# First group's top-k steps behind later u rows, and even and odd attention heads in one step

## The chip, the cores and the metric

The kernel runs on 1 core of a Trainium2 chip. The metric is the device time of one launch in microseconds (us). About 0.5% of it, some 7.6 us, is what a measurement of this kernel can tell from no change.

## The reference

Two transformer-like blocks run one after the other on 256 tokens of width 1024, in float32. The change touches two places of the first block: its attention and the expert layer (`peer`).

```python
def first_block(x, ...):
    xn = rmsnorm(h, norm1_g[layer])
    proj = xn @ w_in[layer]
    q_a, k_a, v_a, q_r, f_r, i_r, g_r = jnp.split(proj, IN_SPLITS, axis=-1)
    attn = moba_attention(q_a, k_a, v_a)      # 8 heads of 64; one block of 256 keys: causal, with a linear bias
    rec = hgrn2(q_r, f_r, i_r, g_r, ...)      # gated recurrence, 4 heads of 128
    h = h + jnp.concatenate([attn, rec], axis=-1) @ w_out[layer]
    hn = rmsnorm(h, norm2_g[layer])
    h = h + peer(hn, peer_wq[layer], peer_subkeys[layer], peer_u[layer], peer_v[layer])

def peer(x, wq, subkeys, u, v):               # per token: 8 heads, 16 experts each
    s = einsum(x @ wq, subkeys)               # 2 x 128 scores for each head
    v1, i1 = top_k(s[:, :, 0], 16); v2, i2 = top_k(s[:, :, 1], 16)
    sc, p = top_k(v1[..., :, None] + v2[..., None, :], 16)
    eidx = take(i1 * 128 + i2, p); gates = softmax(sc)
    act = gelu(einsum(x, u[eidx]))
    return einsum(gates * act, v[eidx])
```

The second block (`second_block`) has a convolution/recurrence layer, an attention layer with 16 heads of 64, and two gated feed-forward layers. It follows the first and is not changed.

## The kernel before

Everything is written by hand for each engine: one program for SyncE (SP, loads of weights), GpSimd (POOL, gathers of expert rows), ScalarE (ACT), VectorE (DVE) and TensorE (PE). The order in which the lines stand is the order in which the engine works; semaphores join the engines.

**First block, attention.** The input projection runs in 14 units of 256 columns. From the ninth on, each unit is cut in halves (`slot_half(s)`, s = 16 to 27, at L1802 and L1805), and PE does other work behind each half. One is the recurrence (`level`, L1920). The other is attention in six steps: i = 0 to 3 for the queries 128 to 255 with two heads each, i = 4 and 5 for the queries 0 to 127 with four heads each. A step is `at_scores` (L1935, in half-unit s = 16 + i), `at_logits`, exponential and `at_norm` on DVE and ACT, `at_transpose` (L1946, s = 18 + i), a copy by ACT (`at_copy`), `at_out` (L1963, s = 20 + i) and `at_store` on DVE (L1215, L1218). Query and key have 64 features a head: an even head lies on partitions 0 to 63, an odd one on 64 to 127. `at_head(i, c)` says which head is the c-th of step i. Before the change all heads of one step have the same parity, so that all its score matmuls read one half of the partitions, all its output matmuls write one half, and its scores stand in one PSUM bank:

```python
return 4 * (i // 2) + i % 2 + 2 * c if i < 4 else (i - 4) + 2 * c
```

DVE also carries the modulation sums of the second block (`ada_ops`, L1098 and L1101) in between, whose weights SP loads (L416).

**End of the projection.** SP loads a unit's weights (L401) once PE is through with the unit four before. When unit 12 is done it starts a long run of loads: the output projection, the last modulation weights (L416), then the first expert query weights (L463), for which the first expert query matmul on PE (L2093) waits.

**Expert layer.** Tokens lie on partitions, 128 at a time (tt = 0, 1). For each of 256 (tile, head, k) one gather brings a row of u for each of the 128 tokens (512 KB), and DVE multiplies and sums it with the activations (`u_row`, L1396). A gather of v goes to PE (`v_row`, L2144), scaled by a diagonal matrix that ACT makes. The gathers are issued by POOL in the order `SEQ` (L540): u rows 0 to 37 first, then u row n and v row n - 38 in turn. They land in a ring of 16 slots, so POOL may be 16 ahead of the consumers (waits on `u_used`, `v_used`, `v_dve`).

The indices of the u rows come in groups of 32 (two heads) out of `top_rows` twice, `top_pairs` and `top_index` on DVE, whose input is the score batch that ACT copies from PSUM (`scores_in`, L732, semaphore `sc_in`). The indices of rows 0 to 31 are there before the row loop starts. Those of the next group (rows 32 to 63) are made between rows 0 and 31, and POOL waits for them at row 32 (`idx_ready`). The row loop calls the four steps behind fixed rows k of the group:

```python
if k == 6:  top_rows(gp + 2, 0, 2)
if k == 9:  top_rows(gp + 2, 2, 4)
if k == 12: top_pairs(gp + 2)
if k == 15: top_index(gp + 2)
```

## Time and profile before

| | us |
|---|---|
| median of 3 runs | 1530.38 |
| lowest and highest | 1525.65, 1531.63 |
| the profiled execution's own time | 1525.67 |
| its span from the first to the last instruction | 1523.8 |
| PE busy | 1366.5 |
| VectorE busy | 1025.8 |

The profile is of one execution, whose own time is close to the lowest of the three. All times in the rows are counted from its first instruction. The stages of the first block are, in that time: projection with recurrence and attention to about 152, output projection and expert queries to about 259 (with the first u rows from 206 on), the gathers of the expert layer to 868, then the second block to the end. "Idle before" in a timeline is idle time of that engine, and the arrow names what ended it.

### The profile page before, as it was taken

What the parts mean: (1) busy time and instruction counts of PE and PEld (TensorE: products, weight loads), DVE (VectorE), ACT (ScalarE), POOL (GpSimd) and SP (SyncE); (2) the same over time, 40 slices, a digit from 0 to 9 for tenths busy, and PEclk for the clock granted to TensorE, in tenths of its full rate; (3) what the DMA queues carried; (4) which work ended last, traced back from release to release, by engine and by line L of the source; (5) the groups of instructions that cost most, each with busy time, mean ns of one, the idle gap of its engine ahead of it and who ended that gap; (6) DMA issues with size and microseconds to landing.
All of it is one profiled execution on the core that took longest, in us unless ns stands there. A gap on an engine that the chain in (4) does not pass through costs nothing.

```text
span 1523.8 us, 20597 instructions
## 1 busy us (share of the span) xinstructions
PE 1366.5 (90%) x7648; PEld 1031.1 (68%) x7648; DVE 1025.8 (67%) x1830; ACT 503.0 (33%) x848; POOL 590.1 (39%) x630
## 2 busy tenths in 40 slices
PE   8999897788877777877788799999999998999998
PEld 7788896244422222322243399999999986999998
DVE  5896769968566676777544567778777467554454
ACT  2222212211111211231212074544445667444342
POOL 1320055777777777777777300022220003000000
PEclk9999999899999999999999999999999999999999
DMA  9865697999999999999999857688883441345540
GB/s 383 316 228 199 229 401 273 419 420 419 419 421 419 420 419 419 420 419 420 419 419 420 350 193 255 218 310 319 320 287 134 165 152 42 125 167 184 187 165 28
DMA packets 114078, 454.16 MB, mean 298 GB/s; under 512 B 12048, under 2 KB 29600, under 8 KB 100816
## 3 DMA queue, kind: packets, MB, share of 16 engines
q0 software_dynamic: 81616, 297.84, 48.8%
q1 hardware_dynamic: 32384, 155.31, 27.9%
q8 instruction: 45, 0.74, 0.2%
q14 instruction: 33, 0.27, 0.0%
HBM read 452.06 MB, written 1.05 MB: 297 GB/s over the span
## 4 chain that ended last, share of the span: by engine, by line
PE 52%; DMA 16%; POOL 12%; DVE 11%; issue 7%; ACT 2%; SPq 0%; DVEq 0%; POOLq 0%; ACTq 0%
PE psum L2253 16%; POOL arena L540 12%; DMA arena<-v_d,arena 10%; PE psum L1862 8%; PE psum L2267 8%; DMA arena<-u_d,arena 5%; DVE arena L1396 3%; PE psum L1818 3%; PE psum L1805 3%; PE psum L2144 2%; PE psum L1893 2%; PE psum L2093 1%; PE psum L1920 1%; PE psum L1877 1%; PE psum L2001 1%
## 5 line engine op out<-in xcount | busy, mean ns | idle before, releaser
L2144 PE MATMUL psum<-arena 128*128 128x512 f32 x952 | 470.1, 621 | 123.6 <-DMA arena<-v_d,arena 107.8
L2144 PEld LDWEIGHTS psum<-arena 128*128 128x128 f32 x952 | 164.6, 191 | 389.9 <-DMA arena<-v_d,arena 247.5
L1396 DVE CUSTOM_DVE_ANT_0 arena<-arena,psum 128x1024 f32<-128x1024 f32 x256 | 306.2, 1219 | 173.0 <-DMA arena<-u_d,arena 172.2
L540 POOL DMA_INDIRECT arena<-u_d,arena x256 | 243.9, 953 | 132.6 <-issue 54.9
L540 POOL DMA_INDIRECT arena<-v_d,arena x256 | 243.3, 950 | 78.1 <-issue 73.2
L1064 DVE TENSOR_TENSOR wlo<-ring,whi 128x2048 fp32r<-128x2048 f32 x69 | 158.1, 2292 | 86.4 <-ACT whi L608 86.4
L775 ACT ACTIVATE arena<-ident,arena 128x128 f32<-128x128 f32 x238 | 89.5, 397 | 353.3 <-PE psum L2144 315.6
L2253 PE MATMUL psum<-xh,whi 128*128 128x256 f32 x704 | 202.3, 287 | 1.6 <-DVE xl L1058 1.4
L2253 PE MATMUL psum<-xl,whi 128*128 128x256 f32 x704 | 199.4, 283 | 0.0
L2253 PE MATMUL psum<-xh,wlo 128*128 128x256 f32 x704 | 199.4, 283 | 0.0
L608 ACT ACTIVATE whi<-ring 128x2048 fp32r<-128x2048 f32 x69 | 131.3, 1903 | 23.6 <-PE psum L1862 18.9
L2253 PEld LDWEIGHTS psum<-xh,whi 128*128 128x128 f32 x704 | 135.1, 192 | 2.6 <-DVE xl L1058 1.8
L2253 PEld LDWEIGHTS psum<-xl,whi 128*128 128x128 f32 x704 | 135.2, 192 | 0.0
L2253 PEld LDWEIGHTS psum<-xh,wlo 128*128 128x128 f32 x704 | 135.1, 192 | 0.0
L555 POOL DMA_DIRECT2D second<-w_ada x64 | 46.3, 724 | 192.0 <-DVE second L1101 115.8
L1079 DVE TENSOR_TENSOR dlo<-ring,dhi 128x1024 fp32r<-128x1024 f32 x44 | 53.9, 1225 | 70.7 <-ACT dhi L624 70.7
L2267 PE MATMUL psum<-fh,dhi 128*128 128x256 f32 x352 | 99.8, 284 | 1.1 <-DVE fl L1644 1.1
L2267 PE MATMUL psum<-fh,dlo 128*128 128x256 f32 x352 | 99.8, 283 | 0.0
L2267 PE MATMUL psum<-fl,dhi 128*128 128x256 f32 x352 | 99.8, 283 | 0.0
L624 ACT ACTIVATE dhi<-ring 128x1024 fp32r<-128x1024 f32 x44 | 46.5, 1058 | 139.0 <-PE psum L2267 139.0
L1862 PE MATMUL psum<-xh,whi 128*128 128x256 f32 x256 | 75.0, 293 | 0.4 <-DVE xl L1058 0.4
L1862 PE MATMUL psum<-xh,wlo 128*128 128x256 f32 x256 | 72.4, 283 | 0.0
(310 smaller groups left out, 2301.0 us busy)
## 6 DMA issues: line engine op xcount, KB each, us to landing
ring<-w_ffn SPq DMA_DIRECT2D x44, 1536.0 KB, 6.8
second<-w_ada POOLq DMA_DIRECT2D x64, 384.0 KB, 6.1
arena<-w_ada SPq DMA_DIRECT2D x50, 384.0 KB, 6.9
ring<-w_inproj SPq DMA_DIRECT2D x14, 1024.0 KB, 7.6
ring<-w_qkv SPq DMA_DIRECT2D x12, 1024.0 KB, 4.9
ring<-w_l0in SPq DMA_DIRECT2D x10, 1024.0 KB, 5.8
ring<-w_peerq SPq DMA_DIRECT2D x6, 1024.0 KB, 8.2
sq<-w_ada SPq DMA_DIRECT2D x14, 384.0 KB, 6.5
```

The lines of the kernel that those rows point to most:

```text
L540: g.indirect_dma_start(S["rows"][:, p % GRING, :], None, u_d if kind == "u" else v_d, bass.IndirectOffsetOnAxis(S["idx"][:, n // SLOTS, n ...
L555: g.dma_start(ada2_slot[i % ADA2_RING].rearrange("p (u c) -> p u c", u=2), ada_weights(1, i)).then_inc(ada2_in[i % ADA2_RING], 16)
L608: a.activation(r32(S[f"whi{g % 2}"]), slot(g, 0, 2048), ACT.Copy).then_inc(w_hi, 1)
L624: a.activation(r32(S[f"dhi{j % 2}"]), slot(g, 2048, 3072), ACT.Copy).then_inc(d_hi, 1)
L775: a.activation(S["diag"][:, c % DIAGS, :], ident[:, :], ACT.Copy, scale=S["wts"][:, n // SLOTS, n % SLOTS:n % SLOTS + 1]).then_inc(diag_re ...
L1064: v.tensor_tensor(r32(S[f"wlo{g % 2}"]), slot(g, 0, 2048), S[f"whi{g % 2}"], ALU.subtract).then_inc(w_lo, 1)
L1079: v.tensor_tensor(r32(S[f"dlo{j % 2}"]), slot(g, 2048, 3072), S[f"dhi{j % 2}"], ALU.subtract).then_inc(d_lo, 1)
L1396: v.tensor_tensor_reduce(row, row, xrow[n // SLOTS], 1.0, 0.0, ALU.mult, ALU.add, S["act"][:, n // SLOTS, n % SLOTS:n % SLOTS + 1]).then_i ...
L1862: ins = t.matmul(bank[g % 2][:, b * T:(b + 1) * T], w(i, b, k), r32((hi, lo)[j][:, k, :]), start=(b == 0 and k == 0 and i + j == 0), stop= ...
L2144: ins = t.matmul(vacc[tt][:, at], S["diag"][:, c % DIAGS, :], row[:, at], start=(n % SLOTS == 0), stop=(n == LAST_PE[tt]))
L2253: ins = t.matmul(bank[g % 2][:, b * T:(b + 1) * T], r32(w[i][:, b, k, :]), r32((xh, xl)[jj][:, k, :]), start=(b == 0 and k == 0 and i + jj ...
L2267: ins = t.matmul(bank[2 + n // 2][:, 256 * (n % 2):256 * (n % 2) + 256], r32(w[i][:, n, :]), r32(S[f"{('fh', 'fl')[jj]}{u % 2}"]), start=( ...
```

## The change

Two things are done.

1. The rows behind which the four top-k steps stand come from a table: (15, 17, 19, 21) for the first group, and (6, 9, 12, 15), as before, for the others.
2. Attention steps take even and odd heads together: step i < 4 the heads 2i and 2i + 1, steps 4 and 5 the heads 0 to 3 and 4 to 7. Scores of even heads go to bank 4 and those of odd heads to bank 5, the transposes to bank 6, the outputs to bank 7. `at_store` copies all 128 partitions at once. The output projection's transposes no longer wait for ACT's last copy. The bias table is laid out from `at_head` as well.

```diff
+TOP_AT = ((15, 17, 19, 21), (6, 9, 12, 15))
...
-    return 4 * (i // 2) + i % 2 + 2 * c if i < 4 else (i - 4) + 2 * c
+    return 2 * i + c if i < 4 else 4 * (i - 4) + c
...
-                a.activation(flat(S[f"PT{i % 2}"]), bank[5][:, :], ACT.Copy).then_inc(at_pt, 1)
+                a.activation(flat(S[f"PT{i % 2}"]), bank[6][:, :], ACT.Copy).then_inc(at_pt, 1)
...
+            def by_parity(ap, i):
+                return ap.rearrange("p (j c n) -> p c j n", c=2, n=T if i < 4 else P)
+
+            def at_banks(i):
+                n = T if i < 4 else P
+                return psum[:, 2048:3072].rearrange("p (c x) -> p c x", c=2)[:, :, 0:T].rearrange(
+                    "p c (j n) -> p c j n", n=n)
...
-                v.tensor_tensor(S[f"L{b}"], bank[4][:, :], S["alibi"][:, i, :], ALU.add).then_inc(at_l, 1)
+                v.tensor_tensor(by_parity(S[f"L{b}"], i), at_banks(i), by_parity(S["alibi"][:, i, :], i), ALU.add
+                                ).then_inc(at_l, 1)
...
-                    v.tensor_copy(S["cat"][p0:p0 + 64, c:c + 2, P:T],
-                                  bank[6][p0:p0 + 64, 0:T].rearrange("p (a t) -> p a t", a=2)).then_inc(at_cat, 1)
+                    v.tensor_copy(S["cat"][:, i, P:T], bank[AT_OUT][:, 0:P]).then_inc(at_cat, 1)
...
-                    v.tensor_copy(S["cat"][p0:p0 + 64, 0:4, 0:P],
-                                  bank[6][p0:p0 + 64, :].rearrange("p (a t) -> p a t", a=4)).then_inc(at_cat, 1)
+                    c = 2 * (i - 4)
+                    v.tensor_copy(S["cat"][:, c:c + 2, 0:P],
+                                  bank[AT_OUT][:, 0:T].rearrange("p (a t) -> p a t", a=2)).then_inc(at_cat, 1)
...
-                    if k == 6:
+                    at = TOP_AT[gp > 0]
+                    if k == at[0]:
                         top_rows(gp + 2, 0, 2)
...
-                    ins = t.matmul(bank[4][:, c * n:(c + 1) * n], S["qa"][p0:p0 + 64, h // 2, q0:q0 + P],
+                    at = c // 2 * n
+                    ins = t.matmul(bank[4 + c % 2][:, at:at + n], S["qa"][p0:p0 + 64, h // 2, q0:q0 + P],
...
-                for c in range(2 if i < 4 else 4):
-                    h = at_head(i, c)
-                    for kt in range(2 if i < 4 else 1):
-                        ins = t.matmul(bank[6][p0:p0 + 64, c * P:(c + 1) * P], S["va"][:, kt, h * HD:(h + 1) * HD],
+                for kt in range(2 if i < 4 else 1):
+                    for c in range(2 if i < 4 else 4):
+                        h = at_head(i, c)
+                        p0, at = 64 * (h % 2), c // 2 * P
+                        ins = t.matmul(bank[AT_OUT][p0:p0 + 64, at:at + P], S["va"][:, kt, h * HD:(h + 1) * HD],
...
                 if tt == 0:
                     pe.wait_ge(at_l, 6)
-                else:
-                    pe.wait_ge(at_pt, 6)
```

DVE in the row loop of the expert layer, before the change, from u row 5 to u row 8. A row is one instruction; `row_in5` is the semaphore of the ring slot in which u row 5 lands, and `sc_in` that of the score batch; MAX and what follows it are `top_rows`:

```order
L1396 ISA arena<-arena,psum 128x1024 [waits row_in5]
L1396 ISA arena 128x1
L1396 ISA arena<-arena,psum 128x1024 [waits row_in6]
L1396 ISA arena 128x1
L1305 MAX arena<-arena 128x8 [waits sc_in]
L1305 MAX arena<-arena 128x8
L1309 MATCH_REPLACE arena<-arena 128x128 [waits dve_seq]
L1310 MAX_INDEX arena<-arena 128x8
L1309 MATCH_REPLACE arena<-arena 128x128
L1311 MAX_INDEX arena<-arena 128x8
L1314 MAX arena<-arena 128x8 [waits dve_seq]
L1314 MAX arena<-arena 128x8
```

The same engine and loop after the change, from u row 14 on:

```order
L1408 ISA arena<-arena,psum 128x1024 [waits row_in14]
L1408 ISA arena 128x1
L1408 ISA arena<-arena,psum 128x1024 [waits row_in15]
L1408 ISA arena 128x1
L1317 MAX arena<-arena 128x8 [waits sc_in]
L1317 MAX arena<-arena 128x8
L1321 MATCH_REPLACE arena<-arena 128x128 [waits dve_seq]
L1322 MAX_INDEX arena<-arena 128x8
```

The wait for the scores has moved from behind u row 6 to behind u row 15.

PE at the end of attention, before: the transposes of the recurrence's result in front of the output projection, the second tile's with a wait for ACT's last attention copy (`at_pt`):

```order
L1989 MATMUL psum<-ident,arena 128x128 [waits at_l,rec_row]
L1989 MATMUL psum<-ident,arena 128x128 x3
L1989 MATMUL psum<-ident,arena 128x128 [waits at_pt,rec_row]
```

The same place after:

```order
L2001 MATMUL psum<-ident,arena 128x128 [waits at_l,rec_row]
L2001 MATMUL psum<-ident,arena 128x128 x3
L2001 MATMUL psum<-ident,arena 128x128 [waits rec_row]
```

Only that wait is gone. In the attention steps themselves PE has the same instructions, in the same places and with the same waits; what differs is the half of the partitions and the bank that each uses, which such rows don't show.

## Rows read from the trace of the kernel before

**Rows 1.** the page: busy time of the matmul engine; GB/s moved in 40 slices
```profile
PE 1366.5 (90%) x7648; PEld 1031.1 (68%) x7648; DVE 1025.8 (67%) x1830; ACT 503.0 (33%) x848; POOL 590.1 (39%) x630
...
GB/s 383 316 228 199 229 401 273 419 420 419 419 421 419 420 419 419 420 419 420 419 419 420 350 193 255 218 310 319 320 287 134 165 152 42 125 167 184 187 165 28
```

**Rows 2.** chain of waits, 80 to 165 us: start, duration, what
```profile
85.93 1.06 PE psum L1935 x4
...
109.64 1.08 PE psum L1935 x8
110.73 1.02 PE psum L1963 x8
...
141.83 1.02 PE psum L1963 x8
...
145.72 6.92 PE psum L1805 x32
...
157.55 14.07 DMA arena<-w_peerq
```

**Rows 3.** stretches: window, sum of busy time, then PE, PEld, DVE, ACT, POOL, clock, DMA
```profile
82.00:122.00 40.00, 40.00 (x224) 33.74 (x223) 37.59 (x64) 13.02 (x40) 10.13 (x7) 1.00 0.58 211
82.00:152.00 70.00, 70.00 (x403) 59.96 (x402) 56.54 (x90) 18.32 (x49) 13.14 (x8) 1.00 0.55 200
142.00:172.00 30.00, 26.13 (x203) 24.96 (x202) 20.37 (x33) 9.82 (x21) 1.13 (x2) 1.00 0.98 371
254.00:868.00 614.00, 490.37 (x1190) 198.98 (x1190) 411.74 (x935) 128.41 (x304) 456.34 (x480) 0.98 1.02 414
```

**Rows 4.** timeline of TensorE in the second block: two heads together, then one alone
```profile
1241.27 0.71 PE L2310 MATMUL psum<-second 64*128 64x256 f32 x4
...
1242.12 0.39 PE L1893 MATMUL psum<-whi,xh 128*128 128x256 f32 x1
...
1249.91 0.70 PE L2310 MATMUL psum<-second 64*128 64x256 f32 x2
...
1250.76 0.48 PE L2336 MATMUL psum<-second 128*128 128x256 f32 x1
```

**Rows 5.** timelines of the attention stage and its end: DVE, PE, SP, PE
```profile
122.33 3.16 DVE L1208 TENSOR_SCALAR arena<-arena 128x128 f32<-128x128 f32 x4
...
128.32 0.60 PE L1946 MATMUL psum<-ident,arena 128*128 128x128 f32 x4
...
141.86 0.34 SPq L401 DMA_DIRECT2D ring<-w_outproj  x1
...
171.66 4.57 PE L2093 MATMUL psum<-xn,arena 128*128 128x128 f32 x24 [3.87 <-DMA arena<-w_peerq]
```

**Rows 6.** timeline of VectorE, first group of u rows: the wait for scores
```profile
214.23 0.08 DVE L1396 DVE_READ_ACCUMULATOR2_ANT arena<- 128x1 f32 x1
224.34 0.49 DVE L1305 MAX8 arena<-arena 128x8 f32<-128x128 f32 x2 [10.03 <-ACT arena L732]
```

**Rows 7.** chain of waits, 224 to 261 us: runs of u rows between top-k steps
```profile
227.22 3.51 DVE arena L1396 x6
...
233.53 3.51 DVE arena L1396 x6
...
242.00 3.51 DVE arena L1396 x6
...
250.88 10.28 DVE arena L1396 x18
```

**Rows 8.** timeline of GpSimd, which issues the gathers
```profile
253.93 0.94 POOL L540 DMA_INDIRECT arena<-u_d,arena  x1 [5.67 <-DVE arena L1396]
255.17 0.94 POOL L540 DMA_INDIRECT arena<-u_d,arena  x1 [0.30 <-issue]
```

**Rows 9.** DMA view, us to landing: u row 15 (issued 210.23), u row 17 (212.72)
```profile
arena<-u_d,arena POOLq DMA_INDIRECT x1, 14.2
...
arena<-u_d,arena POOLq DMA_INDIRECT x1, 16.8
```

More of the change, by code:

```diff
@@ L94 @@
 LEVELS = [128, 64, 32, 16, 8, 4, 2, 1]
+AT_OUT = 7
 def at_head(i, c):
-    return 4 * (i // 2) + i % 2 + 2 * c if i < 4 else (i - 4) + 2 * c
+    return 2 * i + c if i < 4 else 4 * (i - 4) + c
 def build(nc, xT, cols_d, w_d, alibi_d, masks_d, ident_d, tri_d, blk_d, sbmask_d, iota_d, subk_d, rg_d,
@@ L1211, in at_store @@
                 dve.wait_ge(at_o, i + 1)
-                p0 = 64 * (i % 2)
                 if i < 4:
-                    c = 2 * (i // 2)
-                    v.tensor_copy(S["cat"][p0:p0 + 64, c:c + 2, P:T],
-                                  bank[6][p0:p0 + 64, 0:T].rearrange("p (a t) -> p a t", a=2)).then_inc(at_cat, 1)
-                else:
-                    v.tensor_copy(S["cat"][p0:p0 + 64, 0:4, 0:P],
-                                  bank[6][p0:p0 + 64, :].rearrange("p (a t) -> p a t", a=4)).then_inc(at_cat, 1)
+                    v.tensor_copy(S["cat"][:, i, P:T], bank[AT_OUT][:, 0:P]).then_inc(at_cat, 1)
+                else:
+                    c = 2 * (i - 4)
+                    v.tensor_copy(S["cat"][:, c:c + 2, 0:P],
+                                  bank[AT_OUT][:, 0:T].rearrange("p (a t) -> p a t", a=2)).then_inc(at_cat, 1)
             AT_P = [0, 2, 4, 6, 8, 12, 16]
@@ L1480, in _ @@
                 if gp < 7:
-                    if k == 6:
+                    at = TOP_AT[gp > 0]
+                    if k == at[0]:
                         top_rows(gp + 2, 0, 2)
-                    if k == 9:
+                    if k == at[1]:
                         top_rows(gp + 2, 2, 4)
-                    if k == 12:
+                    if k == at[2]:
                         top_pairs(gp + 2)
-                    if k == 15:
+                    if k == at[3]:
                         top_index(gp + 2)
@@ L1945, in at_transpose @@
                 for c in range(4):
-                    ins = t.transpose(bank[5][:, c * P:(c + 1) * P], S[f"P{i % 2}"][:, c * P:(c + 1) * P],
+                    ins = t.transpose(bank[6][:, c * P:(c + 1) * P], S[f"P{i % 2}"][:, c * P:(c + 1) * P],
                                       ident[:, :])
@@ L1958, in at_out @@
                 pt = S[f"PT{i % 2}"]
-                p0 = 64 * (i % 2)
-                for c in range(2 if i < 4 else 4):
-                    h = at_head(i, c)
-                    for kt in range(2 if i < 4 else 1):
-                        ins = t.matmul(bank[6][p0:p0 + 64, c * P:(c + 1) * P], S["va"][:, kt, h * HD:(h + 1) * HD],
+                for kt in range(2 if i < 4 else 1):
[3 more added lines that the diff above has]
+                        ins = t.matmul(bank[AT_OUT][p0:p0 + 64, at:at + P], S["va"][:, kt, h * HD:(h + 1) * HD],
                                        pt[:, 2 * c + kt if i < 4 else c, :], start=(kt == 0), stop=(i >= 4 or kt == 1))
```

## The prediction

> **What bounds the kernel now.** I read the page first, then the chain of waits, then the stretches, and only then the timelines of the two places that the change touches. The page [rows 1] shows TensorE busy for 90% of the span, but the rate at which data moves tells more: from the eighth slice on it stands at 419 to 421 GB/s for 15 slices. That is the expert layer. Between 254 and 868 us the DMA engines are busy all the time [rows 3], and GpSimd issues a gather of 512 KB every 1.24 us [rows 8]. This stretch is a stream: it takes as long as its gathers take, and it starts when the first gather after the last hole is issued. That gather is the one of u row 32, at 253.93 [rows 8]. The seventh slice, 229 to 267 us, with 273 GB/s shows the hole before it.
>
> The attention stage is another matter. In 82 to 152 us TensorE is busy 70.00 of 70.00 us at full clock [rows 3], and the chain of waits runs over it without a break [rows 2]: projection halves, recurrence, scores (L1935), outputs (L1963). When the projection ends, the chain goes over to the load of the first query weights, 14.07 us [rows 2], and TensorE then stands idle for 3.87 us until they are there [rows 5]. Whatever TensorE saves before 152 us starts these loads sooner. The second block follows the stream by data alone and has no clock of its own, so what is won in front stays won.
>
> **The change, part one: the top-k steps.** VectorE ends u row 6 at 214.31 and waits until 224.34 for the scores that ScalarE copies [rows 6]: 10.03 us. Rows 7 to 15 could be worked on meanwhile. A row takes 10.28 / 9 = 1.14 us [rows 7]. After the change rows 7 to 15 would end at 214.3 + 9 x 1.14 = 224.6, but row 15 lands only at 210.23 + 14.2 = 224.4 [rows 9] and so ends at 225.6. The scores are there by then. The four steps take what they take now, read between the runs of rows [rows 6, 7]: 227.22 - 224.34 = 2.88, then 233.53 - 230.73 = 2.80, 242.00 - 237.04 = 4.96, and 250.88 - 245.51 = 5.37 us. So: first step to 228.5; row 16; row 17, which lands at 212.72 + 16.8 = 229.5 [rows 9], to 230.8; second step to 233.6; two rows to 235.9; third step to 240.8; two rows to 243.1; last step to 248.5. Now it ends at 250.88. The index is 2.4 us earlier, not 10, because six more rows (6.9 us) stand in front of it and row 15 lands 1 us late.
>
> The gather of row 32 gains more than its index. It now also waits for 18 rows to be used, which is so at 250.88 + 2 x 1.14 = 253.2, and starts at 253.93. After the change 22 rows are used before the index is there; the gather starts about 0.3 us behind it (the idle time between two gathers, [rows 8]), at 248.8. That is **5.1 us** earlier. The nearest bounds: 2.4 us if the gather follows its index only as late as it does now (some 3 us), and 6.1 us if row 15 is not waited for. I take the middle value, since it has the landings in it. The gathers of rows 22 to 31 come earlier too, and fill the time until about 247 us; they stand behind rows 12 to 21 in the same queue and delay none of them. The loads of the last query weights share the DMA engines with them; nothing in the chain of waits waits for those loads. What follows the index does not hurt: rows 22 to 31 have landed, and VectorE ends row 31 at 260 instead of 269, so that TensorE gets its first scaled v row sooner, which nothing waits for.
>
> **Part two: even and odd heads together.** A pair of score matmuls on different halves of the partitions can run side by side, and the trace has such a pair. In the second block two heads' scores, one on each half, take from 1241.27 to 1242.12, 0.85 us; one head alone takes from 1249.91 to 1250.76, also 0.85 us [rows 4]. The second head is free. Now the attention steps: a score step of two heads is 4 matmuls of 256 columns in 1.06 us, one of four heads 8 of 128 columns in 1.08 us, an output step 8 in 1.02 us [rows 2]. A matmul of 256 columns costs 6.92 / 32 = 0.216 us [rows 2], one of 128 half of it. If half of them are free, a step loses 0.43 us. Scores: 6 x 0.43 = 2.6 us. Outputs: 6 x 0.43 = 2.6 us, but here the two heads share the rows of the array and differ in columns, and no row of this trace shows two such matmuls side by side. Bounds: nothing, or all 2.6. I take all of it, from the nearest row, the pair of scores. TensorE then leaves the stage **5.2 us** sooner. All but the last output step lies before 141.86, where SP starts the run of loads [rows 5]; the run starts 4.8 us sooner, and keeps the DMA engines 98% busy to its end [rows 3]. I take **5.0 us** for the arrival of the query weights. The rest costs nothing: the logits have as many elements from two banks as from one, the copies of `at_store` get shorter (half the elements a partition), and the wait that is dropped was not last.
>
> Beside this stands a page of the Trainium skill, "TensorE: Matmul & The Clock Gate", section "Part 3: Packing small matmuls — row/col tiling", which gives 2.38x for three column tiles. As an estimate from that page, two tiles at the same share of the ideal would give 1.6x, and the outputs 2.0 us instead of 2.6. No row here shows it, and the sum goes without it.
>
> Is VectorE in the way? It is busy 56.54 of 70 us in the stage [rows 3]. The narrowest place that I found is the transpose of step 5: it starts at 128.32, and VectorE is through with its input at 122.33 + 3.16 = 125.49 [rows 5], a margin of 2.8 us. TensorE has by then won 0.43 x 9 = 3.9 us, so VectorE must follow by 1.1 us. Its idle time between 82 and 122 is 40 - 37.59 = 2.4 us [rows 3] and part of this is a wait for TensorE. It just fits; if it did not, up to 1.1 us of the 5.0 would be lost.
>
> **Sum.** 5.1 + 5.0 = 10.1 us. Against the profiled execution: 1525.67 - 10.1 = 1515.6. Its time is 4.7 us below the median of the three runs, so for the median I say 1530.38 - 10.1 = **1520.3 us**.
>
> **Rivals.**
> (a) Outputs do not overlap: only 2.6 us from part two, 7.7 in all, 1522.7. For it: no row shows it. Against: the scores do it fully.
> (b) VectorE or the loads take the bound in the attention stage, and part two gives some 3.5 instead of 5.0: 8.6 in all, 1521.8. For it: the margin of 2.8 us above. Against: VectorE has idle time, and waits for TensorE in this stage more than the other way round.
> (c) The u rows 12 to 17 land later than now, or the index is late, and the gather of row 32 gains only its 2.4 us: 7.4 in all, 1523.0. Row 15 already lands when it is wanted.
> (d) Slower: each change from one half of the array to the other costs a drain. The place is the attention steps. Heads alternate 1 time in four score steps, 3 times in two, and 3 times in each output step, 28 times in all. Going into a 64-wide step and out of it costs 0.85 - 2 x 0.216 - 2 x 0.108 = 0.20 us [rows 2, 4]. At 0.20 us for each of 28 alternations and nothing overlapped, part two costs 5.6 us; against 5.1 gained it ends at 1530.9, 0.5 us above the median. It decides from 0.18 us an alternation. Against it: the pair of scores pays nothing for its alternation [rows 4]. A page of the Trainium skill bears on this, "TensorEngine Tiling (Array Packing)", section "Key Properties": changing the tiling mode drains the engine, changing the tile alone does not. By that rule (d) is out, and the pair in the trace, with its 0.85 us, agrees.
> (e) Part one does nothing, since something other than the index holds gather 32: 5.0 in all, 1525.4. Against it: GpSimd was idle for 5.67 us before that gather, and what ended it was VectorE's work on the rows [rows 8], which part one moves forward.
>
> **How the numbers follow.** Forecast 0.60, (a) 0.15, (b) 0.11, (c) 0.07, (d) 0.03, (e) 0.04. The three runs before spread over 6 us, so a median is good to about 3 us. The range has the forecast with both upper bounds (6.1 + 5.2, less 4 of spread) at its lower end, 1515, and case (e) with some spread at its upper end, 1527. What a measurement can tell from no change is 0.5%, 7.7 us, that is a time under 1522.7. The forecast passes it in most draws, (b) in most, (a) and (c) in half or fewer: faster 0.64, same 0.33, slower 0.03.
>
> **What the profile after would show.** VectorE runs rows 0 to 15 without the wait of 10 us; the first MAX8 comes near 225.6 less the 5 us of part two. The gather of row 32 is issued about 10.1 us before 253.93, near 243.8. Score steps on TensorE take about 0.63 us and output steps 0.6; the first query weights land near 166.6 and the second block starts 10 us sooner. Output steps of 1.0 us would mean (a), idle time of TensorE between 82 and 152 (b), waits of VectorE for u rows 12 to 17 (c), score steps over 1.1 us (d). The prediction is wrong if the stream after row 32 is longer than the 614 us of now, which nothing in the change would explain.

## The result

The changed kernel takes 1516.93 us (median of 7 executions, 1512.38 to 1520.33), the kernel before, run beside it, 1527.67 us (7 executions, 1525.06 to 1531.63). The ratio is 0.9928, with a 95% interval of 0.9913 to 0.9944, which is 11.0 us less (8.6 to 13.3) and more than the 7.6 us that a measurement can tell from no change. The forecast was 10.1 us less and 1520.3 us, so faster, by both parts of the change. A second comparison on another occasion (run e8 below) gave 0.9913 [0.9893, 0.9932].

The profiled execution of the changed kernel has a span of 1517.1 us, where the kernel before had 1523.8. That is only 6.7 us. Why it is less than the medians say the prediction did not see; it has a section of its own below.

The page of the changed kernel, the lines that answer to [rows 1]:

```profile
PE 1364.3 (90%) x7648; PEld 1026.5 (68%) x7648; DVE 1025.8 (68%) x1830; ACT 503.1 (33%) x848; POOL 587.3 (39%) x630
...
GB/s 384 313 234 234 222 419 336 419 420 413 418 421 419 419 420 419 420 420 420 419 419 420 293 215 274 221 320 313 320 270 125 167 136 32 125 167 190 183 166 28
```

TensorE has the same 7648 matmuls and 2.2 us less busy time, and the seventh slice of the span moved 336 GB/s instead of 273: the hole in front of the stream is smaller. The chain of waits through the attention stage, with start, duration and what, answers to [rows 2]:

```profile
86.17 0.63 PE psum L1949 x4
...
108.19 0.65 PE psum L1949 x8
108.83 0.59 PE psum L1977 x8
...
137.34 0.59 PE psum L1977 x8
...
140.80 6.92 PE psum L1818 x32
...
152.85 14.01 DMA arena<-w_peerq
```

A score step of two heads fell from 1.06 to 0.63 us, one of four from 1.08 to 0.65, and an output step from 1.02 to 0.59. The projection half has its 6.92 us as before, and the load of the first query weights is issued at 152.85 instead of 157.55. The stretches, for [rows 3]:

```profile
82.00:122.00 40.00, 40.00 (x247) 33.31 (x246) 38.52 (x68) 13.50 (x40) 10.14 (x8) 1.00 0.60 214
82.00:147.00 65.00, 65.00 (x405) 55.11 (x404) 54.04 (x89) 18.20 (x48) 10.97 (x8) 1.00 0.60 214
244.00:858.00 614.00, 497.19 (x1210) 202.93 (x1210) 408.03 (x927) 129.02 (x305) 455.14 (x480) 0.99 1.02 414
```

TensorE is still busy for all of 82 to 147 us, so nothing of what it saved went into a wait. VectorE went from 37.59 to 38.52 of the first 40 us. From 244 to 858 us the DMA engines are busy all the time, as they were from 254 to 868; from the gather of row 32 to the last gather it takes 601.2 us, before 601.6. Next the timelines of the changed kernel, one engine each: SyncE where the run of loads at the end of the projection begins, TensorE's first query step, VectorE's first and last instruction of the top-k chain, and GpSimd's gathers of u rows 0, 31 and 32 (in brackets the idle time before, and what ended it).

```profile
137.37 0.34 SPq L404 DMA_DIRECT2D ring<-w_outproj  x1
```

```profile
166.91 5.47 PE L2105 MATMUL psum<-xn,arena 128*128 128x128 f32 x32 [4.03 <-DMA arena<-w_peerq]
```

```profile
220.57 0.48 DVE L1317 MAX8 arena<-arena 128x8 f32<-128x128 f32 x2
...
243.39 0.18 DVE L1382 CAST arena<-arena 128x32 int32<-128x32 f32 x1
```

```profile
185.07 1.03 POOL L543 DMA_INDIRECT arena<-u_d,arena  x1 [31.48 <-DVE arena L1382]
...
225.36 0.94 POOL L543 DMA_INDIRECT arena<-u_d,arena  x1 [0.30 <-issue]
243.84 0.94 POOL L543 DMA_INDIRECT arena<-u_d,arena  x1 [17.55 <-DVE arena L1382]
```

The first MAX8 comes at 220.57, which was forecast as 225.6 less the 5 us of part two. The index is ready at 243.58, and the gather of row 32 starts 0.26 us behind it, at 243.84, where 243.8 was forecast and 253.93 stood before [rows 8].

### The profile page after: what moved, and what is told of

Same layout as the page of the kernel before. It is cut to its first block, busy times and chain, and to the rows that moved or that the text cites. A ratio compares the mean times of both kernels' runs of the same rounds, so it can differ in the third digit from the quotient of the medians.

```text
span 1517.1 us, 20596 instructions
## 1 busy us (share of the span) xinstructions
PE 1364.3 (90%) x7648; PEld 1026.5 (68%) x7648; DVE 1025.8 (68%) x1830; ACT 503.1 (33%) x848; POOL 587.3 (39%) x630
## 4 chain that ended last, share of the span: by engine, by line
PE 49%; DMA 20%; DVE 11%; POOL 10%; issue 7%; ACT 1%; SPq 1%; DVEq 0%; POOLq 0%; ACTq 0%
PE psum L2265 16%; POOL arena L543 10%; DMA arena<-u_d,arena 10%; PE psum L1875 9%; PE psum L2279 8%; DMA arena<-v_d,arena 7%; DVE arena L1408 4%; PE psum L1818 3%; PE psum L2156 2%; PE psum L1906 2%; DMA arena<-w_ada 1%; PE psum L1933 1%; PE psum L2105 1%; PE psum L2013 1%; PE psum L1815 1%
## 5 line engine op out<-in xcount | busy, mean ns | idle before, releaser
L611 ACT ACTIVATE whi<-ring 128x2048 fp32r<-128x2048 f32 x69 | 131.3, 1902 | 23.7 <-PE psum L1875 18.9
```

The source lines that it names most:

```text
L611: a.activation(r32(S[f"whi{g % 2}"]), slot(g, 0, 2048), ACT.Copy).then_inc(w_hi, 1)
```

## The experiments

All kernels ran beside the kernel before; a median stands against that of before in the same comparison. Absolute times of two profiles can't be subtracted to better than some 3 us, since the profiled executions reach the attention stage at different times: the first score step starts at 84.07 us in one of the 14 profiles (e4) and at 87.25 in another (e10). Two distances are used instead. One is from the first score step to the first query step on TensorE: 85.8 us in both profiles of the kernel before, 80.5 to 81.2 wherever even and odd heads go together and nothing is added in between. The other is from the gather of u row 0 to that of row 32 on GpSimd: 64.1 us in each of the three profiles with the old top-k rows, 58.8 in the profile of the changed kernel. The second one is not fixed: over the seven profiles with the top-k steps behind rows 15, 17, 19 and 21 it goes from 58.6 to 60.2 us (58.8 after, 59.5 in e8, 60.2 in e5, 58.6 to 58.9 in the others), and what varies is how long VectorE waits for rows 13 to 15 to land.

### Each part alone

e1 is the kernel before with the first part alone:

```diff
+TOP_AT = ((15, 17, 19, 21), (6, 9, 12, 15))
...
-                    if k == 6:
+                    at = TOP_AT[gp > 0]
+                    if k == at[0]:
                         top_rows(gp + 2, 0, 2)
```

> The kernel before with the first change alone: the top-k steps of the first group stand behind u rows 15, 17, 19 and 21, the attention steps are as before. Theory 1 (the two parts add, and the first is worth what its wait for row 15's landing takes away): the gather of u row 32 starts at 248.6 us of the profile instead of 253.93, the gather of row 0 stays at 189.8, and the time is 5.1 to 5.4 us under before (ratio 0.9966). Rival (the first part only pays since the gathers start 4.75 us earlier in the changed kernel, with other landings): the gather of row 32 moves by under 3 us, and the time by under 3 us. If before loses TensorE clock in the second block's attention in some executions, this kernel has both levels of time too.

e2 is the changed kernel without it:

```diff
-TOP_AT = ((15, 17, 19, 21), (6, 9, 12, 15))
+TOP_AT = ((6, 9, 12, 15), (6, 9, 12, 15))
```

> The changed kernel with the first group's top-k steps back behind u rows 6, 9, 12 and 15: only the attention with even and odd heads together is left of the change. Theory 1: score steps 0.63 to 0.65 us and output steps 0.59 us as in the changed kernel, gather of row 0 at 185.1 us, gather of row 32 at about 249.2 us (4.75 us before 253.93), time 4.7 to 5.2 us under before (ratio 0.9968). Rival (without the later rows the top-k chain waits for the landings of row 15 in another way, and eats part of it): gather of row 32 at over 251 us, time under 3 us below before.

e1 took 1523.11 us against 1529.35 (ratio 0.9956 [0.9942, 0.9971], so 6.7 us less, 4.4 to 8.9), e2 1524.92 (0.9978 [0.9963, 0.9993], 3.4 us less, 1.1 to 5.7). The timelines of GpSimd with the gathers of rows 0 and 32, e1 first, then e2:

```profile
188.57 1.03 POOL L542 DMA_INDIRECT arena<-u_d,arena  x1 [31.21 <-DVE arena L1372]
...
247.44 0.94 POOL L542 DMA_INDIRECT arena<-u_d,arena  x1 [17.64 <-DVE arena L1372]
```

```profile
183.69 1.03 POOL L543 DMA_INDIRECT arena<-u_d,arena  x1 [31.70 <-DVE arena L1382]
...
247.79 0.93 POOL L543 DMA_INDIRECT arena<-u_d,arena  x1 [5.67 <-DVE arena L1408]
```

With the top-k part alone the distance is 247.44 - 188.57 = 58.87 us, with the heads alone 247.79 - 183.69 = 64.10, exactly as before. So the first part is worth 5.2 us here and 5.3 in the changed kernel, whether or not the gathers begin earlier, and the second part does nothing there. (With the other profiles of the same top-k rows it is 3.9 to 5.5 us, by the landings.) From the first score step to the first query step it is the other way round: 85.88 us in e1 and 81.02 in e2, 4.8 less than before. The parts add: 5.2 and 4.8 us by these distances. The two ratios add up to 10.1 us as well, but each of them is good to 2.3 us only.

The absolute times that were expected for the two profiles were missed by 1.2 to 1.4 us (gather of row 0 at 188.57 instead of 189.8 in e1, at 183.69 instead of 185.1 in e2), since both executions reached the first score step earlier, at 84.71 and 84.50 us instead of 85.86.

### Does the order within an output step matter?

In the changed kernel neighbouring output matmuls of the first four steps belong to an even and an odd head. e5 orders them by head, with the same halves and the same banks:

```diff
-                for kt in range(2 if i < 4 else 1):
-                    for c in range(2 if i < 4 else 4):
+                for c in (0, 1) if i < 4 else (0, 2, 1, 3):
+                    for kt in range(2 if i < 4 else 1):
```

> The changed kernel with the output matmuls of an attention step ordered by head, the even heads' first and then the odd heads', so that neighbours in the order mostly share a half of the array's columns; which bank and which half each writes is unchanged. Theory A (only neighbours in the order overlap): of 8 matmuls 1 pair or so overlaps, an output step takes 0.9 to 1.0 us instead of 0.59, and the six steps are 1.8 to 2.6 us longer. Rival B (the order within a step does not matter, since the queue in front of the array is deep enough): 0.59 to 0.65 us.

Its chain of waits:

```profile
112.46 0.59 PE psum L1977 x8
```

0.59 us, as with alternation, in all six steps. Theory A fell. In the program the first matmul of the odd head stands behind four matrix passes of the even one (each of these fp32 matmuls shows as two). In the records of single matmuls of the first output step the first two start at 107.061 and 107.074, 0.013 us apart, and the other passes go on in such pairs, one pair every 0.109 us; before the change single passes start 0.109 us apart. The records don't name the half that a matmul uses, so that the two of a pair are one of each head is concluded from this pairing. By it the halves are fed side by side even across four passes. What had kept them apart before was not the order within a step but that all heads of a step shared one half. (The one execution took 1521.01 us. Its profile has a 10.2 us fall of the clock, see below, and its gather of row 32 comes 60.16 us behind that of row 0, since row 13 landed late.)

### How far forward can the index go?

In the changed kernel VectorE does two rows between each pair of top-k steps. By the time the second step is done, all these rows have landed, so they could as well come after the index. e3 puts the last two steps behind row 17:

```diff
-TOP_AT = ((15, 17, 19, 21), (6, 9, 12, 15))
+TOP_AT = ((15, 17, 17, 17), (6, 9, 12, 15))
```

> The changed kernel with the last two top-k steps behind u row 17 instead of rows 19 and 21 (15, 17, 17, 17): the index is asked for after 18 rows instead of 22. Theory A (from row 15 on the vector engine works through its rows without a wait, so each row taken out from in front of the index brings it forward by the row's own 1.2 us): index ready at about 239 us instead of 243.6, gather of u row 32 at about 239.3 us, and the whole stream 4.5 us earlier, so 4 to 5 us under the changed kernel (about 1512.5). Rival B (GpSimd's later gathers, or the landings, then set the start): the gather of row 32 moves by under 2 us and the time stays within 2 us of the changed kernel's. Rival C: TensorE has less to do while it waits and loses clock at 256 us and after, which gives back 1 to 3 us.

e6 puts all four behind row 14:

```diff
+TOP_AT = ((14, 14, 14, 14), (6, 9, 12, 15))
```

> The changed kernel with all four top-k steps of the first group behind row 14. Theory A (the gather of u row 32 also waits until the vector engine has used the first rows of its ring, and rows 15 to 17 now come behind the index): the index is ready some 3.4 us earlier than behind row 17, counted from the gather of row 0, but the gather of row 32 starts 53.5 to 55 us behind that of row 0, as it did there (54.0), and the time is no better than 1510.8. Rival B (only the index holds that gather): 50.0 to 51.0 us behind the gather of row 0, and the time 3 us lower still.

Timelines of VectorE (the index) and GpSimd (the gather of row 32) in e3:

```profile
236.55 0.18 DVE L1382 CAST arena<-arena 128x32 int32<-128x32 f32 x1
```

```profile
183.00 1.03 POOL L543 DMA_INDIRECT arena<-u_d,arena  x1 [31.24 <-DVE arena L1382]
...
237.00 0.94 POOL L543 DMA_INDIRECT arena<-u_d,arena  x1 [12.77 <-DVE arena L1382]
```

And in e6, with the gathers of rows 0, 30, 31 and 32:

```profile
234.17 0.18 DVE L1382 CAST arena<-arena 128x32 int32<-128x32 f32 x1
```

```profile
183.67 1.02 POOL L543 DMA_INDIRECT arena<-u_d,arena  x1 [31.81 <-DVE arena L1382]
...
235.86 0.94 POOL L543 DMA_INDIRECT arena<-u_d,arena  x1 [13.39 <-DVE arena L1408]
237.10 0.94 POOL L543 DMA_INDIRECT arena<-u_d,arena  x1 [0.30 <-issue]
238.64 0.94 POOL L543 DMA_INDIRECT arena<-u_d,arena  x1 [0.60 <-issue]
```

In e3 the distance between the two gathers is 54.00 us, 4.77 less than in the changed kernel's profile. From the first MAX8 to the index it is 18.4 us instead of 23.0, and these 4.6 us are the four rows of 1.14 us taken out from in front of the index; the other 0.2 us are landings. The median is 1512.58 us, ratio 0.9896 [0.9877, 0.9916]. Theory A holds by the gathers, and B does not. The ratio fits too, but alone it doesn't tell e3 from the changed kernel, since its interval overlaps that of the second comparison. C is not borne out in its size: the fall of the clock at 254.6 us lasts as long as in the changed kernel (6.8 us). Nor does the stream behind it give anything back: from the gather of row 32 to the last one it takes 600.9 us, in the changed kernel 601.2. In e6 the index is ready 50.7 us behind the gather of row 0 (234.35 - 183.67) instead of 53.7 in e3, but the gather of row 32 starts at 54.97: it now waits for VectorE to use rows 15 to 17. GpSimd stands still for 13.39 us in front of the gather of row 30 until VectorE is through with row 15, the gather of row 31 comes only at 237.10, and that of row 32 starts 0.77 us behind the end of row 17 (237.87), as it did before the change. Row 17 is where the two conditions meet. That is theory A as well, with one number missed: e6 took 1508.61 us in its single execution, less than the 1510.8 that A allowed, since this execution had no fall of the clock in the second block. By its gathers (the last one starts 656.1 us behind the first, in e3 654.9) it is 1.2 us worse than e3.

## What the profiled executions hide: a fall of the clock in the second block

The second block's feed-forward steps start at 965.85 us before and at 954.44 after: 11.4 us sooner. 9.9 of these are the two parts (the last gather of the stream lands at 868.30 and 858.37). The rest, 1.5 us, is in a step at the end of the stream, in the chains of waits of before and of after:

```profile
872.49 3.54 PE psum L2168 x16
```

```profile
862.56 2.05 PE psum L2180 x16
```

The first profile of the kernel before, and the second too, had the clock at 0.5 there for 3.4 us, and neither profile of the changed kernel had. This is no gain of the change: e3, e5 and e12 have that fall as well (5 of 14 profiles). At the end of the kernel only 6.7 us of the 11.4 are left. The stretches around the second block's attention show where 4.7 went, with the granted clock as the last but two of the columns; first after, then before, then a second profile of the kernel before (run e11):

```profile
1250.00:1260.00 10.00, 9.01 (x25) 6.35 (x26) 5.56 (x12) 5.01 (x10) 2.68 (x3) 0.50 0.44 157
```

```profile
1262.00:1272.00 10.00, 9.35 (x48) 7.01 (x48) 7.67 (x16) 7.73 (x16) 4.01 (x4) 1.00 0.36 141
```

```profile
1262.00:1272.00 10.00, 10.00 (x29) 6.92 (x29) 5.00 (x11) 3.87 (x8) 2.39 (x3) 0.50 0.34 138
```

> The kernel before once more, for its profile. Its first profile was of an execution of 1525.67 us and had no fall of the clock behind its own empty stretch of 2.36 us (1260.0 to 1262.4), and 18 of its 23 timed executions beside the second set of kernels lie at 1528.1 to 1532.1, five at 1523.7 to 1525.3. Theory 1 (the upper group has the fall): time 1528 to 1532 and the clock at 0.5 for 6.8 to 10.2 us from about 1262 us; or, with one chance in five, time 1524 to 1526 and no fall. Rival (the groups come from elsewhere): 1528 to 1532 without a fall in that place.

The granted clock is 0.50, that is 1.2 GHz instead of 2.4, over nearly the same work, in the profile after and in the second one of before, and 1.00 in the first one of before. e11 took 1531.46 us, the execution of the first profile 1525.67; the fall in e11 lasted 13.7 us, longer than the 6.8 to 10.2 expected. What TensorE did just before is the same in all three, in the timelines of before, of e11 and of after:

```profile
1262.40 0.70 PE L2336 MATMUL psum<-second 128*128 128x256 f32 x2 [2.36 <-DVE second L1732]
```

```profile
1261.82 1.22 PE L2336 MATMUL psum<-second 128*128 128x256 f32 x2 [2.36 <-DVE second L1732]
```

```profile
1250.99 0.80 PE L2348 MATMUL psum<-second 128*128 128x256 f32 x1 [2.35 <-DVE second L1745]
```

It had no work for 2.35 us, since it waited for VectorE, and VectorE was behind because of one long instruction, the split of an output weight (here of the changed kernel):

```profile
1247.12 2.29 DVE L1067 TENSOR_TENSOR wlo<-ring,whi 128x2048 fp32r<-128x2048 f32 x1 [0.86 <-ACT whi L611]
...
1250.38 0.56 DVE L1745 TENSOR_TENSOR second<-second 128x384 f32<-128x384 f32 x1
```

Three kernels put 14 matmuls of 128 by 256 (into a bank that is started anew afterwards, results not used) at three places around that stretch. e4 has them ahead of the after-step of head 3, e9 behind it, e10 behind that of head 4:

```diff
+                if h == 4:
+                    for i in range(14):
+                        t.matmul(bank[0][:, 0:T], r32(xh[:, i % KT, 0:P]), r32(xh[:, i % KT, :]),
+                                 start=True, stop=True, skip_group_check=True)
                 if h - 1 < SBH:
                     z_after(h - 1)
```

> The changed kernel with 14 matmuls (128 by 256, into a bank that is started anew afterwards) put ahead of the third head's after-step in the second block's attention, where TensorE had 2.35 us without work before its granted clock fell to 0.5 for 10.2 us in the changed kernel's profile. Their results are not used. Theory 1 (the empty stretch is what the clock fell for, and it cost 4.7 us in the profile): the granted clock stays at 1.00 from 1245 to 1300 us, the matmuls fit into the empty stretch, the time between the start of the second block's feed-forward steps and the end of that attention is what it is in the kernel before, and the median is 2 to 5 us under the changed kernel's, with no cluster of slower executions. Rival (the fall has nothing to do with that stretch): the clock still falls in some execution, the time stays within 1 us of the changed kernel's or is up to 1.5 us longer for the added matmuls.

> The changed kernel with the same 14 matmuls right behind the third head's after-step instead of ahead of it: the same work, but TensorE's empty stretch of about 2.4 us stays. Theory 1 (it is the empty stretch that the clock falls for): the fall behind it is there as in the changed kernel, and the time is 0 to 2 us above the changed kernel's (16 to 19 us of matmul time at most 1.5 to 3 us). Rival (more matmuls anywhere in that stage hold the clock, or the shift of the later steps does): no fall in the profile, median within 1.5 us of the 1513.2 of the kernel with the matmuls in front.

> The changed kernel with the same 14 matmuls behind the fourth head's after-step, that is behind TensorE's empty stretch of 2.35 us in the second block's attention, which so stays (ahead of it and behind the third head's after-step, the 14 matmuls had cut it to 0.83 and 0.69 us). Theory 1 (the fall of the granted clock follows on that stretch): stretch 2.3 to 2.4 us, the clock at 0.5 from about its end for 3.4 to 10.2 us, median 1515 to 1518, as the changed kernel's or up to 1.5 us above. Rival (it is the amount of matmul work in the stage, not where it stands): no fall, median within 1.5 us of 1513.

> The changed kernel once more, unchanged, for the comparison in the same call: if the clock falls behind TensorE's empty stretch in the second block's attention in most executions and not in all, the profile has either none (span about 1512 to 1513) or a fall of 3.4 to 10.2 us (1515 to 1520), and the median is 2.5 to 5 us above that of the kernel with the matmuls in front.

I had put the matmuls of e4 one head too early: the empty stretch stands before the after-step of head 4, not of head 3. In the timelines of TensorE of e4, e9 and e10 the added matmuls (L2385, L2387) and the after-step of head 4 (L2348) read:

```profile
1243.04 1.94 PE L2385 MATMUL psum<-xh 128*128 128x256 f32 x14
...
1248.33 0.70 PE L2348 MATMUL psum<-second 128*128 128x256 f32 x2 [0.83 <-DVE second L1745]
```

```profile
1247.32 1.91 PE L2387 MATMUL psum<-xh 128*128 128x256 f32 x14
...
1251.57 0.70 PE L2348 MATMUL psum<-second 128*128 128x256 f32 x2 [0.69 <-DVE second L1745]
```

```profile
1253.16 0.70 PE L2348 MATMUL psum<-second 128*128 128x256 f32 x2 [2.36 <-DVE second L1745]
...
1254.06 1.80 PE L2387 MATMUL psum<-xh 128*128 128x256 f32 x13
```

Both e4 and e9 have the matmuls in front of the stretch, and since VectorE's work goes on meanwhile, both cut it, to 0.83 and 0.69 us. From the first after-step to that of head 4 it takes 13.5 us in both, as without them: the matmuls cost nothing there. So e9 was no control, and its expectation failed by its own premise. e10 is the control: the stretch keeps its 2.36 us.

Over all profiles taken for this study (span less the start of the last gather is the time of all that comes behind the stream):

```
kernel                empty stretch   clock at 0.5 there       last gather to end
before                2.36 us         none                     668.2 us *
before, again (e11)   2.36            13.7 us                  674.4 *
e1                    2.36            10.2                     672.4
e2                    2.37             3.4                     668.8
changed               2.35            10.2                     672.1
changed, again (e8)   2.36             6.8                     671.0
e3                    2.36            10.2                     673.3 *
e5                    2.36            10.2                     673.6 *
e6                    2.36            none                     667.0
e10                   2.36            none                     669.6 (14 matmuls in the way)
e4                    0.83            none                     666.9
e9                    0.69            none                     666.5
e7                    0.84            none                     667.0
e12                   0.83            none                     667.6 *

* with the 3.4 us fall at the end of the stream (1.5 us in the first row)
```

With the empty stretch the clock fell in 7 of 10 profiles, without it in none of 4. The fall began between 1.0 us before the end of the stretch and 1.5 us behind it. It costs about half of its length, 2 to 6 us. This is shown as a price. As a cause it is supported and not settled: e10, the one control, was expected to show the fall in its profile and did not, and if the filling did nothing, 7 falls spread over 14 profiles would miss just those four in 1 case of 29. The times lean the same way in part. e4 took 1513.19 us (1511.58 to 1514.05) and e10 1517.37 (1515.44 to 1519.16), where the changed kernel spread from 1511.85 to 1520.35 over 13 executions with medians 1516.93 and 1515.39. But e9, with the stretch filled, took 1515.30 (1514.94 to 1516.29), no less than the changed kernel in the same comparison (e8, 1515.39). The 2.5 to 5 us that were expected between the changed kernel and a filled one are 2.2 against e4, which ran on another occasion, and 0.1 against e9. e9's profile has no fall in the second block; it starts its gathers 2.9 us later than e4 does (185.59 and 182.72), by a later first score step and a longer fall in front of the query step. The second profile of the changed kernel has a fall of 6.8 us and 1516.58 us, as was expected. The ratios of e4, 0.9902 [0.9884, 0.9920], and of the changed kernel overlap, so what the filling is worth on the median is somewhere from nothing to 5 us.

The fall explains how the two numbers of the result go together. The kernel before was profiled in an execution without the fall and the changed one in an execution with it, so the spans show 6.7 us. The medians show 11.0. That most of the timed executions of both have the fall is likely from the profiles (1 of 2 before, 2 of 2 after, 7 of all 10) and from the two groups of times that the kernel before has (18 of 23 executions beside e1 to e4 at 1528.1 to 1532.1 us, 5 at 1523.7 to 1525.3), but not shown. Nor is this fall all that tells executions apart: the start of the first score step goes over 3.2 us and the landings of rows 13 to 15 over 1.5 us, and why they do was not looked into.

### The same in front of the query weights, and both fixes together

e7 has the steps of e3 and the matmuls of e4. e12 has in addition 28 matmuls ahead of the wait for the first query weights:

```diff
                 if tt == 0:
-                    query_landed(pe, j)
                     pe.wait_ge(rec_cat, 8)
+                    if j == 0:
+                        for _ in range(28):
+                            t.matmul(at[:, 0:P], ident[:, :], ident[:, :], start=True, stop=True,
+                                     skip_group_check=True)
+                    query_landed(pe, j)
```

> The changed kernel with the top-k steps behind rows 15, 17, 17, 17 and with the 14 added matmuls ahead of the third head's after-step. Theory (the two are apart, 700 us from each other): gather of u row 32 comes 54.0 us behind the gather of row 0 (58.8 in the changed kernel), clock at 1.00 from 1235 to 1300 us, median 4.5 us under the one with the matmuls alone (1513.2), so about 1508.7. Rival (the lowest time is set by something common, such as the clock drops in the first 450 us, which fall elsewhere): the median stays over 1511.

> The kernel with both fixes and, besides, 28 matmuls of 128 by 128 ahead of the wait for the first query weights, where TensorE had 4.0 us without work and every profile shows the clock at 0.5 for 3.4 to 6.8 us behind it. Theory 1 (a stretch without work is what the clock falls for, and filling it helps anywhere): no fall between 160 and 175 us, the first query step takes 3.7 us instead of 5.5, the gathers start 1.5 to 2 us earlier against the landing of the weights, median about 1507. Rival A (the clock falls anyway, since TensorE is little used in the whole stretch): the fall stays and the time is 1508.5 to 1509.5. Rival B (the added matmuls run into the landing and delay the query step by up to 1 us): 1509.5 to 1510.

e7 took 1508.98 us (1507.79 to 1511.44), ratio 0.9868 [0.9850, 0.9885]: 20 us under the kernel before, and clear of both of the changed kernel's intervals. No version here was measured to be faster (e12 has the same median, and e6, with 1508.61, has one execution). Its distance between the gathers of rows 0 and 32 is 54.03 us, as expected. e12 took 1508.98 us as well (0.9883 [0.9861, 0.9905]). TensorE at the query step, e7 first:

```profile
168.17 6.16 PE L2105 MATMUL psum<-xn,arena 128*128 128x128 f32 x32 [4.28 <-DMA arena<-w_peerq]
```

```profile
160.74 6.42 PE L2102 MATMUL psum<-ident 128*128 128x128 f32 x56
167.00 3.74 PE L2109 MATMUL psum<-xn,arena 128*128 128x128 f32 x32
```

Without the filling all 13 other profiles have the clock at 0.5 for 3.4 to 6.8 us within 163 to 176 us, in or behind an empty stretch of 3.7 to 4.4 us, and the query step takes 5.3 to 6.6 us; with it the clock stays up and the step takes 3.7. But the 28 matmuls took 6.4 us (each of fp32 goes through in two passes, x56). The weights were issued at 150.8 and landed 14.0 us later, at 164.8, and the step could only start at 167.00. From the first score step to the query step it takes 82.9 us, where e7 has 81.1, and from there to the gather of row 0 16.4 instead of 18.9 (18.2 where the fall is short). Together that is 99.3 us, where e7 has 99.9 and the profiles of the changed attention with a short fall have 98.7 to 99.3. So what the clock gave back, the overrun took: theory 1 held for the clock but not for the time. What rival B describes happened, by 2 us instead of up to 1; the median, 1508.98, is under the 1509.5 that B gave and equal to e7's. It is one profile, and a filling of half the length was not tried.

## Why the prediction was right, point by point

**What bounds the kernel.** The reading held. The stream has the same 414 GB/s over an equal 614 us, and what both parts saved reached the end of the kernel as a shift of what stands in front of it.

**Part one, 5.1 us forecast.** The gathers of rows 0 and 32 are 58.77 us apart instead of 64.10, 5.3 us less, and e1 alone has 5.2. That these agree so well with 5.1 is in part luck: e8, the same kernel again, has 59.51 us (4.6 less), and e5, with the same top-k steps, 60.16 (3.9 less). Both conditions that were told apart are seen: the idle time of GpSimd before that gather is ended by the index, which stands 0.26 us ahead of it (0.3 forecast). The landings did hold VectorE, as the text had it, by 0.8 us instead of its 1: rows 13 and 14 made it wait, and row 15, issued at 205.48, landed 13.9 us later, at 219.4, just when VectorE was through with row 14. The first MAX8 follows at 220.57. In e5 the waits for landings come to 2.2 us and in e8 to 1.6. The DMA view of the changed kernel, for the gather issued at 205.48:

```profile
arena<-u_d,arena POOLq DMA_INDIRECT x1, 13.9
```

The six rows behind it still stood in front of the index as the text counted them, and e3 shows that four of those were not needed, 4.6 us that neither the change nor the prediction took up.

**Part two, 5.0 us forecast.** Score steps 0.63 to 0.65 us (0.63 forecast), output steps 0.59 (0.6 forecast), 12 steps by 0.43 = 5.2 us for TensorE. (What the text counts as 4 matmuls of 256 columns are 2 matmuls in two passes each; the sum is not touched by that.) The loads were issued 157.55 - 152.85 = 4.7 us sooner and the gathers of rows 0 to 15 started 4.75 us sooner; the first score step was itself 0.2 us later in this profile, so it is 4.9 to 5.0. The value taken for the outputs, all of it from the pair of scores in the second block, was the open end of the sum. It was taken without a row for it, and it came out right: in these steps matmuls that share the rows of the array and differ in columns overlap as fully as those that share the columns, 0.43 us a step in both. The page "TensorE: Matmul & The Clock Gate" of the Trainium skill, section "Part 3: Packing small matmuls — row/col tiling", gives 2.38x for three column tiles, from which the estimate of 2.0 us for this term came; the trace has 6 x 0.43 = 2.6, so the row was the better guide. By the rule of the Trainium skill, "TensorEngine Tiling (Array Packing)", section "Key Properties", changing the tiling mode drains the engine and changing the tile alone does not; the 0.59 us of every output step, in the changed kernel and in e5, agree with the second half of it.

**VectorE's margin.** The place named was the transpose of step 5. After the change VectorE's input and TensorE's transposes of steps 4 and 5 stand like this:

```profile
119.53 3.39 DVE L1222 TENSOR_SCALAR arena<-arena 128x128 f32<-128x128 f32 x4
```

```profile
120.02 0.60 PE L1960 MATMUL psum<-ident,arena 128*128 128x128 f32 x4
...
124.69 0.60 PE L1960 MATMUL psum<-ident,arena 128*128 128x128 f32 x4
```

VectorE is through at 122.92 and the transpose starts at 124.69: a margin of 1.8 us is left of 2.8. VectorE followed by 2.6 us, where 1.1 were needed. It fitted, as the text said. TensorE was 65.00 of 65.00 us busy, so rival (b) did not occur.

**The rivals.** (a) is refuted by the 0.59 us, (d) by every step, (e) by e1 alone. (c) did not come true, by the gather at 243.84, but its mechanism is real: in e5 VectorE waits 1.97 us for row 13, and the gather of row 32 is 1.4 us later against that of row 0 than in the changed kernel's profile. The timeline of VectorE in e5:

```profile
217.35 1.22 DVE L1408 CUSTOM_DVE_ANT_0 arena<-arena,psum 128x1024 f32<-128x1024 f32 x1 [1.97 <-DMA arena<-u_d,arena]
```

**The median.** It was forecast as 1520.3 from a median of three of 1530.38; the median of before turned out to be 1527.67 in this comparison and 1528.4 to 1529.4 in the later ones, and the measured 1516.93 lies 3.4 us under the forecast for that reason more than for the size of the gain, 11.0 instead of 10.1 us, whose interval holds both. What the text did not have is why single executions of one kernel differ by 5 to 8 us, of which the fall of the clock is a large part. It said that the second block has no clock of its own, so that what is won in front stays won. In the medians that was so. For a single profile it was wrong: the second block has the fall of TensorE's clock, which can take 2 to 6 us. It made the profiled spans differ by 6.7 us only, and by the text's own sum for the profiled execution (1515.6 us; measured 1518.93) the forecast was 3.3 us off.

## What to carry to other kernels

Put small matmuls that use different halves of the array into one step, by rows or by columns: in both cases the second half was free here, and the order within the step was not what decided. When a queue of gathers waits for an index, list both what the index waits for and what the ring waits for, and put just as many rows in front as the ring needs; that was four fewer than the change left there. Read such a distance in more than one profile of the same kernel, since the landings in it vary. And before two profiles are subtracted, compare the granted clock stretch by stretch: one fall of the clock cost 2 to 6 us here, and each part of the edit brought 5.

## What the runs showed of the hardware

- Output matmuls of 64 columns on different column halves: 8 in 0.59 us where 8 on one half took 1.02. With the order by head the first two passes start 0.013 us apart, as the others do in pairs, though four passes of one half stand ahead of the first of the other in the program.
- At an empty stretch of 2.35 us TensorE's granted clock fell to 0.5 in 7 of 10 profiles, for 3.4 to 13.7 us, and with 0.69 to 0.84 us left of it in none of 4. At one of 3.7 to 4.4 us it fell in 13 of 13, and with that stretch filled in the single profile taken it did not.
- The same gathers land differently from one execution to the next: rows 13 to 15 held VectorE for 0.6 to 2.2 us in all over ten profiles.
- 14 matmuls put ahead of an empty stretch cost nothing in time (13.5 us from the first after-step to the fourth head's with and without them), since the engine that is waited for goes on.
- 28 matmuls of fp32, 128 by 128, took 6.4 us, 0.23 us each.
